# Feed-forward products of four groups as seven block products, with weight sums made by adding transfers

## The reference

```python
D_FF = 2816
def swiglu(h, w_in, w_out):          # h [512, 1024], w_in [1024, 5632], w_out [2816, 1024]
    gu = h @ w_in
    return (jax.nn.silu(gu[..., :D_FF]) * gu[..., D_FF:]) @ w_out
...
x = x + swiglu(rmsnorm(x, norm_ffn[i]), ffn_w_in[i], ffn_w_out[i])    # i = 0, 1
```

## Time and profile before

| | |
|---|---|
| runs | 2080.11, 2080.69, 2082.20 us; median 2080.69 |
| profiled execution, span | 2080.3 us |
| mean granted TensorE clock | 0.997 |
| TensorE busy | 2041.6 us, 98% |
| VectorE busy | 965.7 us, 46% |
| ScalarE busy | 780.6 us, 38% |
| GpSimd busy | 324.6 us, 16% |
| moved by transfers | 187.32 MB, mean 90 GB/s |

### The profile page before, as it was taken

How to read it: one execution, slowest core, us unless ns; L and a number is a source line. 1 busy time by engine, 2 the same in 40 slices (tenths; PEclk the granted TensorE clock), 3 DMA queues, 4 the chain that set the end, 5 groups by cost and what they waited for, 6 DMA issues and landing times.

```text
span 2080.3 us, 26716 instructions
## 1 busy us (share of the span) xinstructions
PE 2041.6 (98%) x10149; PEld 1656.0 (80%) x10149; DVE 965.7 (46%) x1969; ACT 780.6 (38%) x1552; POOL 324.6 (16%) x497
## 2 busy tenths in 40 slices
PE   7999999999999999999999999999998999999998
PEld 6887888888888886788888888888787888777766
DVE  5437434443354345435534443364435664535455
ACT  4226332222232222333322222243337884435453
POOL 1103100000011120000110000041003764312211
PEclk9999999999999999999999999999999999999999
DMA  5330243333324331133243333225321103423212
GB/s 179 104 99 11 63 133 95 99 91 101 93 81 142 91 101 41 53 99 97 69 132 99 97 96 99 93 83 160 119 75 58 32 22 102 114 74 109 66 47 81
DMA packets 96910, 187.32 MB, mean 90 GB/s; under 512 B 8423, under 2 KB 16655, under 8 KB 96656
## 3 DMA queue, kind: packets, MB, share of 16 engines
q1 hardware_dynamic: 90432, 164.35, 26.3%
q0 software_dynamic: 6352, 21.27, 3.2%
HBM read 181.33 MB, written 4.26 MB: 89 GB/s over the span
## 4 chain that ended last, share of the span: by engine, by line
PE 90%; ACT 5%; DVE 2%; issue 1%; POOL 1%; DMA 0%; SPq 0%; ACTq 0%; DVEq 0%; POOLq 0%
PE bank L754 62%; PE bank L790 9%; PE bank L1265 5%; PE bank L1024 2%; PE bank L1186 1%; PE bank L1163 1%; PE bank L828 1%; PE bank L1279 1%; ACT sc L1808 1%; PE bank L1009 1%; PE bank L1095 1%; PE bank L1302 1%; PE bank L853 1%; ACT xn L1802 1%; PE bank L1152 1%
## 5 line engine op out<-in xcount | busy, mean ns | idle before, releaser
L1979 DVE TENSOR_TENSOR wl<-raw,wh 128x1024 fp32r<-128x1024 f32 x306 | 376.7, 1235 | 771.9 <-ACT wh L1382 770.9
L1382 ACT ACTIVATE wh<-raw 128x1024 fp32r<-128x1024 f32 x306 | 320.9, 1053 | 827.3 <-PE bank L754 785.5
L754 PE MATMUL bank<-hTh,wh 128*128 128x512 f32 (+2 forms) x1200 | 467.5, 390 | 0.2 <-issue 0.2
L754 PE MATMUL bank<-hTl,wh 128*128 128x512 f32 (+2 forms) x1200 | 466.9, 389 | 0.0
L754 PE MATMUL bank<-hTh,wl 128*128 128x512 f32 (+2 forms) x1200 | 466.9, 389 | 0.0
L754 PEld LDWEIGHTS bank<-hTh,wh 128*128 128x128 f32 (+2 forms) x1200 | 223.9, 187 | 48.7 <-issue 0.3
L754 PEld LDWEIGHTS bank<-hTh,wl 128*128 128x128 f32 (+2 forms) x1200 | 223.9, 187 | 48.2
L754 PEld LDWEIGHTS bank<-hTl,wh 128*128 128x128 f32 (+2 forms) x1200 | 223.9, 187 | 47.9
L754 PE MATMUL bank<-wh,hTh 128*128 128x512 f32 x400 | 156.5, 391 | 0.1
L754 PE MATMUL bank<-wh,hTl 128*128 128x512 f32 x400 | 155.7, 389 | 0.0
L754 PE MATMUL bank<-wl,hTh 128*128 128x512 f32 x400 | 155.6, 389 | 0.0
(11 more groups left out here) (383 smaller groups left out, 3105.5 us busy)
## 6 DMA issues: line engine op xcount, KB each, us to landing
raw<-in_ffn_w_in SPq DMA_DIRECT2D x88, 512.0 KB, 3.7
raw<-in_ret_w_in SPq DMA_DIRECT2D x48, 512.0 KB, 3.8
raw<-in_ffn_w_out SPq DMA_DIRECT2D x44, 512.0 KB, 3.7
raw<-in_diff_w_in SPq DMA_DIRECT2D x32, 512.0 KB, 3.7
raw<-in_fox_w_in SPq DMA_DIRECT2D x24, 512.0 KB, 4.1
raw<-in_nsa_w_in SPq DMA_DIRECT2D x20, 512.0 KB, 3.7
raw<-in_ret_w_out SPq DMA_DIRECT2D x16, 512.0 KB, 3.7
raw<-in_fox_w_out SPq DMA_DIRECT2D x8, 512.0 KB, 3.7
```

Source lines behind the costliest of these rows:

```text
L754: i = pe.do.matmul(dst, x, y, start=first and k == 0 and q == 0, stop=stop)
L1382: act.do.activation(M.hl[n % HL_SLOTS][0][:, 0:m], M.raw[n % RAW_SLOTS][:, 0:m], ACT.Copy).then_inc(*T.up("act_hi", n))
L1979: dve.do.tensor_tensor(wl[:, 0:m], M.raw[n % RAW_SLOTS][:, 0:m], wh[:, 0:m].bitcast(F32), ALU.subtract).then_inc(*T.up("dve_lo", n))
```

## The change

Take the operand A of a group's down product (512 tokens by 512 features) and its weight block B (512 features by 1024 columns), each cut into quadrants A11, A12, A21, A22 and B11, B12, B21, B22. A quadrant of A is 256 tokens by 256 features, one of B is 256 features by 512 columns, which is one chunk. Before, the product took eight products of quadrants, and each chunk served 24 matmuls. Now, for groups 1 to 4 (`SEVENS`), it takes seven: four of A's operands are sums (S1 to S4) and four of B's are sums (U1 to U4), after Winograd. Each serves 12 matmuls. Groups 0 and 5 are left as they were.

- **TensorE** (`pe_seven`): seven steps of two row blocks `r`. The steps accumulate in banks X, W and Y (two banks each) in the order X, W, X, Y, W, Y, Y. A step that comes back to a bank goes on adding to it, and waits until VectorE has read the bank's earlier value (`dve_seven`).
- **VectorE**: `sums` makes S1, S3, S2, S4 in place in `pr`, each waiting for the one before. `low` makes the low parts of the three new sums and of S3. `evict` reads each step's two banks into `x`, or the first step's into a sum `alpha`. After the last group `merge` adds `alpha` to six half rows of `x`. The `al` and `ah` work of the first two tiles of a group is cut to half width.
- **ScalarE**: `high` rounds the four sums, and it splits seven chunks in place of four, as VectorE does.
- **Weights**: three quadrants B11, B22, B21 are loaded as before. U1 = B11 + B12, U2 = U1 + B22, U4 = U2 + B21 and U3 = B22 + B12 (the signs are taken care of on the side of A) are not loaded: GpSimd issues a transfer that adds another quadrant from HBM into the `raw` buffer that holds the first (`pool_added`). U1, U2 and U4 are made one from the other in the buffer of B11, U3 in that of B22. Each addition waits until both splits of the buffer's former content are done. The buffer of B11 comes free for the next load when U4 is split, that of B22 when U3 is split.

```diff
+SEVENS = (1, 2, 3, 4)
+STEPS = (("X", "A11"), ("W", "S1"), ("X", "A12"), ("Y", "S2"), ("W", "S4"), ("Y", "S3"), ("Y", "A22"))
+INTO = ("alpha", (2, 1, -1), (0, 0, 1), (0, 1, -1), (0, 1, -1), (2, 1, -1), (2, 0, 1))
+ADDED = {"U1": ("B11", "B12", "B11"), "U2": ("B11", "B22", "U1"), "U3": ("B22", "B12", "B22"), "U4": ("B11", "B21", "U2")}
+QUADS = ("B11", "B22", "B21")
+SEVEN = ("B11", "U1", "B21", "U2", "B22", "U3", "U4")
+HELD = {"B11": "U4", "B22": "U3", "B21": "B21"}
...
         if n >= RAW_SLOTS:
-            sp.wait_ge(*at("act_hi", n - RAW_SLOTS))
-            sp.wait_ge(*at("dve_lo", n - RAW_SLOTS))
+            last = LOADS[n - RAW_SLOTS][4]
+            sp.wait_ge(*at("act_hi", last))
+            sp.wait_ge(*at("dve_lo", last))
...
+def pool_added(pool, T, M, i, g):
+    where, first, blocks = BLOCKS[f"ffo{i}", FFG[g][0]]
+    for form in SEVEN:
+        if form not in ADDED:
+            continue
+        home, more, of = ADDED[form]
...
+        pool.wait_ge(*T.at("act_hi", n))
+        pool.wait_ge(*T.at("dve_lo", n))
...
+        pool.do.dma_start(dst, src, accum_op=ALU.add).then_inc(*T.up(f"add{form}", first, step=16))
...
+def pe_seven(pe, T, M, tag, operand, ready):
+    first4, next4 = pe.banks4(), pe.banks4()
+    banks = T.bank[tag] = {"X": first4[0:2], "Y": first4[2:4], "W": next4[0:2]}
+    seen = {}
+    for j, (where, form) in enumerate(STEPS):
...
+        for r in range(2):
+            b, cols = banks[where][r], slice(r * 128, r * 128 + 128)
+            if where in seen:
+                pe.wait_ge(*T.at("dve_seven", (tag, seen[where], r)))
...
+            pe_weights(pe, T, n)
...
# act_ffn
+        splits = 7 if g - 1 in SEVENS else FFG[g - 1][1] // 128
+        for c in range(splits):
+            if g in SEVENS and c < 2:
+                for form in (("S1", "S3"), ("S2", "S4"))[c]:
+                    high(g, form)
+            act_split(act, T, M)
...
# dve_ffn
+        if g in SEVENS:
+            sums(g)
+        if g - 1 in SEVENS:
+            for j in range(7):
+                if g in SEVENS and j < 2:
+                    for form in (("S1", "S3"), ("S2", "S4"))[j]:
+                        low(g, form)
+                for r in range(2):
+                    evict(g - 1, j, r)
+                dve_split(dve, T, M)
+            continue
```

More of the change, by code:

```diff
@@ L70, with plain, seven @@
 FFG = [(0, 256)] + [(256 + g * 512, 512) for g in range(5)]
-def weight_chunks():
-    chunks = []
+SEVENS = (1, 2, 3, 4)
[5 more added lines that the diff above has]
+HELD = {"B11": "U4", "B22": "U3", "B21": "B21"}
+def weight_chunks():
+    loads, chunks, added = [], [], {}
+    def plain(name, r0, nk, cols):
+        chunks.append((nk, sum(n for _, n in cols), len(loads), None, None))
+        loads.append((name, r0, nk, cols, len(chunks) - 1))
+    def seven(name, r0, rows, halves):
+        first, n = len(loads), len(chunks)
+        where = {q: first + k for k, q in enumerate(QUADS)}
+        last = {q: n + SEVEN.index(HELD[q]) for q in QUADS}
+        blocks = {q: (name, r0 + rows * (int(q[1]) - 1), rows // 128, (halves[int(q[2]) - 1],)) for q in ("B11", "B12", "B21", "B22")}
+        for q in QUADS:
+            loads.append((*blocks[q], last[q]))
+        added[name, r0] = (where, n, blocks)
+        for form in SEVEN:
+            chunks.append((rows // 128, halves[0][1], where, form, n))
     def block8(name, *cols):
@@ L110, in weight_chunks @@
             for r0 in range(g * 512, g * 512 + 512, 256):
-                chunks.append(("reto", r0, 2, ((half * 512, 512),)))
+                plain("reto", r0, 2, ((half * 512, 512),))
     ffn(1)
@@ L352, in chunk_views, with chunk_source, chunk_loaded @@
 def chunk_views(M, n):
-    _, _, nk, cols = CHUNKS[n]
-    width = sum(k for _, k in cols)
+    nk, width = CHUNKS[n][0:2]
     return [x[:, 0:nk * width].rearrange("p (t n) -> p t n", t=nk) for x in M.hl[n % HL_SLOTS]] + [nk]
+def chunk_source(M, n):
+    nk, width, where, form, _ = CHUNKS[n]
+    if form is None:
+        return M.raw[where % RAW_SLOTS][:, 0:nk * width]
+    return M.raw[where[ADDED[form][0] if form in ADDED else form] % RAW_SLOTS][:, 0:nk * width]
+def chunk_loaded(T, n):
+    _, _, where, form, first = CHUNKS[n]
+    if form in ADDED:
+        return T.at(f"add{form}", first)
+    load = where if form is None else where[form]
+    return T.at(f"raw{load % RAW_SLOTS}", load)
 def query(M, h):
@@ new lines, in low, with evict @@
+    def low(g, form):
+        h, l = seven_form(f, g, form)
+        dve.wait_ge(*at("act_s", (i, g, form)))
+        dve.do.tensor_tensor(l, seven_sum(f, form), h.bitcast(F32), ALU.subtract).then_inc(*up("dve_s", (i, g, form)))
+    def evict(g, j, r):
+        tag = f"down{i}{g}"
+        where = STEPS[j][0]
+        src = M.bank[T.bank[tag][where][r]][:, :]
+        dve.wait_ge(*at("pe_product", (tag, j, r)))
+        if INTO[j] == "alpha":
+            if g == SEVENS[0]:
+                dve.do.tensor_copy(f.alpha[:, r, :], src).then_inc(*up("dve_seven", (tag, j, r)))
+            else:
+                dve.wait_ge(*at("dve_seven", (f"down{i}{g - 1}", j, r)))
+                dve.do.tensor_tensor(f.alpha[:, r, :], f.alpha[:, r, :], src, ALU.add).then_inc(*up("dve_seven", (tag, j, r)))
+            return
+        t, half = INTO[j][0] + r, INTO[j][1]
+        xs = M.X[:, t, half * 512:half * 512 + 512]
+        dve_x_newest(dve, T, t)
+        dve.do.tensor_tensor(xs, xs, src, ALU.add if INTO[j][2] > 0 else ALU.subtract).then_inc(*up("dve_seven", (tag, j, r)))
+        dve.x[t] = ("seven", (tag, j, r))
@@ L2241, in dve_ffn, with merge @@
+    def merge(t):
+        r, tag = t % 2, f"down{i}{SEVENS[-1]}"
+        dve.wait_ge(*at("dve_seven", (tag, 0, r)))
+        for half in ((1,), (0, 1))[t // 2]:
+            xs = M.X[:, t, half * 512:half * 512 + 512]
+            dve_x_newest(dve, T, t)
+            dve.do.tensor_tensor(xs, xs, f.alpha[:, r, :], ALU.subtract if half else ALU.add).then_inc(*up("dve_x", (f"merge{i}", t, half)))
+            dve.x[t] = (f"merge{i}", t, half)
     for t in late[1]:
@@ L2250, in dve_ffn @@
         dve_product(dve, T, M, 4, 4, take_up(g))
+        if g in SEVENS:
+            sums(g)
+        if g - 1 in SEVENS:
+            for j in range(7):
[6 more added lines that the diff above has]
+            continue
         for half in range(2):
             dve_product(dve, T, M, FFG[g - 1][1] // 256, 4, dve_add(dve, T, M, f"down{i}{g - 1} {half}", half))
+            if g in SEVENS:
+                for form in (("S1", "S3"), ("S2", "S4"))[half]:
+                    low(g, form)
+    for t in range(4):
+        merge(t)
     if i == 0:
```

106 lines of the change are left out of this document (86 added, 20 removed).

## The result

| | before | after |
|---|---|---|
| median of runs | 2081.28 us (4 runs, 2080.11 to 2082.20) | 2171.95 us (4 runs, 2169.76 to 2175.96) |
| profiled execution, span | 2080.3 us | 2168.5 us |
| mean granted TensorE clock | 0.997 | 0.980 |

The ratio is 1.0434, with a 95% interval of 1.0421 to 1.0446: slower by 4.3%. The span grew by 88.2 us, and 81 had been predicted.

The account below looks back on a forecast made before the run. TensorE, busy 98%, bounds the kernel before; in the new products VectorE's list and waits for transfers do. Each group takes 32.1 us against 22.0, 10.1 more; eight give 81, so 2080.3 + 81 = 2161 us, range 2122 to 2222.

Parts of the forecast that it names:

- What is removed: All eight groups' down products: 12 of 96 matmuls fewer, 2.75 us a group, 22.0 us in all.
- Steps 1 to 3: Steady group up to bank X's first reading: U1, U2, B22's split, sums; TensorE's third step at 12.4 after 6.9 us idle.
- Steps 4 and 5: Rest of the group: U3, U4's split, reload of B11's buffer; seventh step at 29.35, group 32.1 us against 22.0.
- T: Adding transfer by GpSimd, issue to landing: 4.8 us plain load plus 1.7 for second read, 6.5 us; bounds 4.0 and 9.
- the prediction's own ends: Group length at other adding-transfer times: 27.6 us at 4.0, 28.45 at 4.8, 39.6 at 9.
- the first fall: TensorE's clock after 6.9 us idle before the third step: 3.1 us lost each group, but hidden.
- the second fall: Clock falling again at 2.9 us idle before the seventh step: 3.1 us a group, 25 us; in a rival of chance 0.25.
- GpSimd's descriptors: VectorE's two-input operations hold back writing of U3's descriptors: 3.9 us a group, 31 us; in a rival of chance 0.25.
- The change pays: Rival: whole kernel at 2058 us and a little, if bank X's first reading lands under 5.5; chance 0.03.

Follow-up runs that it names:

- experiment 7: Changed kernel with sums last, sixth wh/wl pair, earlier splits, fifth raw buffer, plus VectorE's readings ahead of non-urgent splits: 2071.83 us, ratio 0.9951.
- experiment 1: Changed kernel with the four adding transfers made plain overwriting transfers, sums of weight blocks left out: 2137.14 us, ratio 1.0268.
- experiment 4: Changed kernel with unread filling matmuls ahead of TensorE's third and seventh steps, two versions: 2170.38 and 2171.14 us, ratios 1.0428 and 1.0430.
- experiment 2: Changed kernel with sums, roundings and low parts moved behind the last reading of the seven before: 2167.20 us, ratio 1.0412.
- experiments 7 and 8: The second is the kernel of experiment 7 with each tile's merge put just ahead of that tile's additions in down(5): 2071.74 us, ratio 0.9956.

## Why the prediction was right, step by step

**What is removed.** 2.75 us a group. With the waits gone, the sevens gave back 19.5 of 22.0 us (experiment 7).

**Steps 1 to 3.** U1 at ScalarE at -12.2 (442.00; said: -12.2), U2 at -3.4 (450.83; said: -3.25), the split of B22 until 7.4 (said: 7.6), TensorE's third step at 12.06 after 6.4 us idle (said: 12.4 and 6.9). Right to 0.5 us.

**Steps 4 and 5.** U3's issue at 7.97 (said: 7.65), its split at 15.03 (15.3), U4's split until 19.8 (20.1), the load's reader on VectorE at 24.5 (25.0), the seventh step at 28.75 (29.35). Right, each a little early. Their end was not: 33.1 instead of 32.1.

**T.** The prediction called T the time from issue to landing, but its steps count it from the end of the split that frees the buffer. Measured that way it is 6.5 us, as said: B22's split ends at 461.64, GpSimd issues 0.54 us later, the transfer takes 5.95, and its reader starts at 468.15; U1 and U2 take 6.54 and 6.52. Both parts of the sum come out too: without the add (experiment 1) the same link takes 4.6 (said: 4.8), and the add costs 1.9 (said: 1.7). At 4.6 the prediction's own ends give about 28.2 us a group, 3.9 less than at 6.5; 4.35 less was measured, and the kernel takes 2137 us where the sum gives about 2130. Part of what is missing may again be the clock: the mean was 0.987, and in seven of experiment 1's eight groups a step took 3.8 to 5.1 us instead of 2.75.

**The clock.** The prediction hid the first fall, rightly in group 2: the fourth step ended near 473.3, and VectorE read it only at 476.25. It left the second fall, at 2.9 us idle, to a rival at 25 us. It came in five of the eight groups, at 1.1 to 1.7 us each, and not at 3.1; in the last group of each feed-forward the sixth step was slow instead (4.45 us). In group 2 the seventh step started 0.6 us earlier than said and took 1.6 longer, which gives 33.1 for 32.1. So most of the total of +88 instead of +81 is a fall of the clock that the sum had at nothing, partly offset by steps that came a little early. Within the profile of the changed kernel two neighbours show its price: group 3's seventh step started at +28.69, like group 2's, kept the full clock, and its seven took 31.57 us instead of 33.10. Against that stands experiment 4, which kept the clock up at that step and gained nothing, so what the falls cost the whole kernel stays open.

**The rivals.** GpSimd's descriptors were not held back: U3 took 5.95 us from its issue while VectorE made the sums, and U2 of the same group took as long (444.87 to 450.82) while VectorE stood still for most of it. That agrees with the Trainium skill's "SBUF — State Buffer" (who interferes with whom), by which two-input VectorE operations disturb only reads of GpSimd. "The change pays" was rightly refused on VectorE's list as it stood, and its condition was the right one: the first reading of X under 5.5. Taking the sums away alone (experiment 2) left that reading at 7.4 and brought 4.8 us. With all splits one chunk earlier as well, a fifth raw buffer and the new order (experiment 7) it starts at 4.1, the third step waits for nothing, and the change pays. What the prediction did not see is that two buffers and an order would allow it.

## What to carry to other kernels

The longest idle time in the profile is not the one to remove: 3.9 of the 6.4 us before the third step taken away brought 4.8 us in the whole kernel, since a transfer further back set the end anyway. When fewer matmuls come with more dependent small steps, write down the chain from buffer to buffer and give it one more slot at its narrowest place before touching the arithmetic: one pair of buffers and splits one chunk earlier gave 75 of the 90 us. And what a busy helper engine is spared in one stage can show up in the next (experiments 7 and 8).

## What was not expected of the hardware

- A transfer of 512 KB issued by GpSimd takes 4.1 us to land, with an add 6.0; its issue holds GpSimd for 0.72 and 1.20 us. From the end of the split that it waits for to its issue another 0.5 to 0.6 us pass. Issued right behind another it lands 8.0 to 8.6 us after its issue.
- The granted clock went to 0.50 in a pause of 2.95 us that followed at least 10 us at the full clock, and the matmuls stood 0.23 us apart again about 3.4 us after work began anew; the earlier trace rows had shown 6.2 us after a pause of 4.8. A pause of 2.92 us left the clock up in the next group, and one of 1.86 us in group 4, with one of 1.62 shortly before it, did not.
- An adding transfer with nothing visibly beside it took 7.5 us in one place of the kernel with filling matmuls, and 5.95 in the changed kernel at the same place. No run tells why.
